# Turning four tiles of an input projection: weight slices stationary, 256 tokens moving

## The reference, cut to what matters

```
h = rmsnorm(x, mix_pre_g)                      # 256 x 2048
proj = h @ w_in                                # 2048 -> 5 * 1024
q, f_logit, i, g, u = split(proj, 5)           # 1024 columns each
f = lb + (1 - lb) * sigmoid(f_logit)           # forget gate, per channel
k = 1 - f
S_t = diag(f_t) S_{t-1} + k_t^T i_t            # 8 heads of 128 channels
o_t = S_t^T q_t
y_rec = rmsnorm(o, g_norm) * silu(g)
```

## Time and profile before

| what | value |
|---|---|
| median of the 3 runs | 1878.26 us |
| lowest and highest | 1876.82 and 1879.6 us |
| profiled execution, first to last instruction | 1875.8 us |
| PE busy in it | 1837.3 us (98%), 8386 matmuls and as many weight loads |
| DVE, ACT, POOL busy | 951.9, 804.5, 49.6 us |
| mean granted TensorE clock | 0.994 of full |

### The profile page before, as it was taken

How to read it: one execution, slowest core, us unless ns; L and a number is a source line. 1 busy time by engine, 2 the same in 40 slices (tenths; PEclk the granted TensorE clock), 3 DMA queues, 4 the chain that set the end, 5 groups by cost and what they waited for, 6 DMA issues and landing times.

```text
span 1875.8 us, 21635 instructions
## 1 busy us (share of the span) xinstructions
PE 1837.3 (98%) x8386; PEld 1525.8 (81%) x8386; DVE 951.9 (51%) x965; ACT 804.5 (43%) x926; POOL 49.6 (3%) x110
## 2 busy tenths in 40 slices
PE   7999999999999999999999999999999999999997
PEld 6888888888788887788888877888888888788886
DVE  4544445544444444655745456445444544444544
ACT  5444444444433434643234445444444444433432
POOL 0000000000000000250000000000000000000000
PEclk9999999999999999999999999999999999999998
DMA  7665656556566656455443554555555655555552
GB/s 263 189 198 180 196 183 192 188 186 194 194 198 191 197 186 199 158 184 176 135 135 131 200 185 149 188 191 189 183 197 182 198 179 191 208 185 201 186 194 90
DMA packets 145438, 344.68 MB, mean 184 GB/s; under 512 B 5400, under 2 KB 5472, under 8 KB 145008
## 3 DMA queue, kind: packets, MB, share of 16 engines
q1 hardware_dynamic: 144544, 339.77, 55.4%
q0 software_dynamic: 736, 4.26, 0.6%
q10 hardware_dynamic: 112, 0.03, 0.0%
HBM read 341.94 MB, written 2.10 MB: 183 GB/s over the span
## 4 chain that ended last, share of the span: by engine, by line
PE 97%; DVE 1%; ACT 1%; POOL 0%; issue 0%; DMA 0%; DVEq 0%; SPq 0%; POOLq 0%; ACTq 0%; PEldq 0%
PE ps L729 31%; PE ps L731 31%; PE ps L730 31%; PE ps L801 1%; PE ps L891 1%; PE ps L783 1%; DVE x L562 0%; PE ps L928 0%; ACT ps L311 0%; DMA x<-in_x_dram 0%; POOL hrr L282 0%; PE ps L918 0%; PE ps L879 0%; DVE xT_lo L488 0%; ACT xT_hi L318 0%
## 5 line engine op out<-in xcount | busy, mean ns | idle before, releaser
L481 DVE TENSOR_TENSOR wlo<-raw,whi 128x1024 fp32r<-128x1024 f32 x640 | 783.0, 1226 | 844.3 <-ACT whi L299 840.3
L299 ACT ACTIVATE whi<-raw 128x1024 fp32r<-128x1024 f32 x640 | 677.7, 1060 | 919.8 <-PE ps L731 918.8
L729 PE MATMUL ps<-whi,xT_hi 128*128 128x512 f32 x1728 | 680.5, 394 | 6.7 <-DVE wlo L481 4.4
L731 PE MATMUL ps<-whi,xT_lo 128*128 128x512 f32 x1728 | 674.9, 391 | 0.0
L730 PE MATMUL ps<-wlo,xT_hi 128*128 128x512 f32 x1728 | 674.6, 390 | 0.0
L729 PEld LDWEIGHTS ps<-whi,xT_hi 128*128 128x128 f32 x1728 | 325.8, 189 | 73.8 <-issue 4.8
L731 PEld LDWEIGHTS ps<-whi,xT_lo 128*128 128x128 f32 x1728 | 325.7, 188 | 68.7
L730 PEld LDWEIGHTS ps<-wlo,xT_hi 128*128 128x128 f32 x1728 | 326.1, 189 | 66.1
L729 PE MATMUL ps<-whi,hT_hi 128*128 128x512 f32 x832 | 324.5, 390 | 2.0 <-PEq L936 1.6
L731 PE MATMUL ps<-whi,hT_lo 128*128 128x512 f32 x832 | 323.7, 389 | 0.0
L730 PE MATMUL ps<-wlo,hT_hi 128*128 128x512 f32 x832 | 323.7, 389 | 0.0
(11 more groups left out here) (99 smaller groups left out, 365.7 us busy)
## 6 DMA issues: line engine op xcount, KB each, us to landing
raw<-in_ffn_w_gate_dram SPq DMA_DIRECT2D x88, 1024.0 KB, 5.2
raw<-in_ffn_w_up_dram SPq DMA_DIRECT2D x88, 1024.0 KB, 5.2
raw<-in_ffn_w_down_dram SPq DMA_DIRECT2D x88, 1024.0 KB, 5.2
raw<-in_w_in_dram SPq DMA_DIRECT2D x40, 1024.0 KB, 5.1
raw<-in_w_out_dram SPq DMA_DIRECT2D x16, 1024.0 KB, 4.9
x<-in_x_dram SPq DMA_DIRECT2D x4, 512.0 KB, 9.3
gpost<-in_ffn_post_g_dram POOLq DMA_DIRECT2D x2, 1024.0 KB, 5.0
out_dram<-x SPq DMA_DIRECT2D x4, 512.0 KB, 2.9
```

The lines of the kernel that those rows point to most:

```text
L299: nc.scalar.activation(whi[:, g % RING, :], raw[:, g // 2 % RAW, 1024 * (g % 2):1024 * (g % 2 + 1)], ACT.Copy).then_inc(hi_ready, 1)
L481: V.tensor_tensor(wlo[:, g % RING, :], raw[:, g // 2 % RAW, 1024 * (g % 2):1024 * (g % 2 + 1)], whi[:, g % RING, :].bitcast(f32), ALU.subt ...
L729: mm(bank, a_hi, whi[:, s, c0:c0 + NT], start=start, stop=False)
L731: return mm(bank, a_lo, whi[:, s, c0:c0 + NT], start=False, stop=stop)
```

## The change

The four first tiles are computed by a new function on PE, with the roles of the operands exchanged: a 128 by 128 slice of `whi` or `wlo` is stationary, and the 256 tokens of `xT_hi` or `xT_lo` move. A half is 24 matmuls of 256 columns. The result has channels on the partitions. The copy into `nat`, the transposes and their evacuation by ACT go for these tiles; DVE takes the banks out, times `rb`, which holds the inverse roots of all 256 tokens on every partition. `rb` is made once: DVE writes `diag` (the identity times each token's root), PE multiplies it by ones (one float32 matmul, 256 columns), ACT copies it out. The sigmoid runs on `T` in place.

```diff
+            def turned_half(g, n, banks):
+                pe.wait_ge(lo_ready, g + 1)
+                s = g % RING
+                for c in range(2):
+                    k = 2 * n + c
+                    for q in range(4):
+                        dst = banks[q // 2][:, SEQ * (q % 2):SEQ * (q % 2 + 1)]
+                        cols = slice(c * NT + P * q, c * NT + P * (q + 1))
+                        mm(dst, whi[:, s, cols], xT_hi[:, k, :], start=k == 0 and q % 2 == 0, stop=False,
+                           skip_group_check=True)
+                        mm(dst, whi[:, s, cols], xT_lo[:, k, :], start=False, stop=False, skip_group_check=True)
+                        ins = mm(dst, wlo[:, s, cols], xT_hi[:, k, :], start=False, stop=k == KC - 1,
+                                 skip_group_check=True)
+                ins.then_inc(w_used, 1)
...
# PE
-                if h == 0 and t >= 2:
-                    pe.wait_ge(nat_ok, 2 * (t - 1))
-                narrow_half(IN + p, 0, h, ps[2 * (t % 2):2 * (t % 2) + 2])
-                if 1 <= t <= 4 and h == 2:
-                    pe.wait_ge(nat_ok, 2 * t)
-                    if t > 1:
-                        pe.wait_ge(in_ev, 2 * (t - 1))
-                    transpose_tile(nat, 0, (4, 5), in_tr, False)
+                if h == 0 and 2 <= t < 6:
+                    pe.wait_ge(in_free, t - 1)
+                if h == 0 and t >= 6:
+                    pe.wait_ge(nat_ok, 2 * (t - 5))
+                if t < 4:
+                    turned_half(IN + p, h, ps[2 * (t % 2):2 * (t % 2) + 2])
+                else:
+                    narrow_half(IN + p, 0, h, ps[2 * (t % 2):2 * (t % 2) + 2])
+                if p == 11:
+                    pe.wait_ge(ones_ok, 1)
+                    pe.wait_ge(diag_ok, 1)
+                    mm(ps[4][:, 0:SEQ], ones[:], diag[:], start=True, stop=True).then_inc(rb_mm, 1)
...
# ACT
-                if 1 <= t <= 4 and h == 4:
-                    act.wait_ge(in_tr, t)
-                    dst, fn = (T, ACT.Sigmoid) if t <= 2 else (qP, ACT.Copy)
-                    h0 = 4 * ((t - 1) % 2)
-                    for c in range(2):
-                        nc.scalar.activation(flat(dst[:, h0 + 2 * c:h0 + 2 * c + 2, :]), ps[4 + c][:],
-                                             fn).then_inc(in_ev, 1)
+                if p == 12:
+                    act.wait_ge(rb_mm, 1)
+                    nc.scalar.activation(rb[:], ps[4][:, 0:SEQ], ACT.Copy).then_inc(rb_ok, 1)
+                if p in (15, 19):
+                    h0 = 0 if p == 15 else 4
+                    for c in range(2):
+                        act.wait_ge(in_tr, h0 // 2 + c + 1)
+                        part = flat(T[:, h0 + 2 * c:h0 + 2 * c + 2, :])
+                        nc.scalar.activation(part, part, ACT.Sigmoid).then_inc(in_ev, 1)
...
-                if h == 7:
+                if h == 7 and t >= 4:
...
# DVE
-                if t in (1, 2) and h == 5:
-                    dve.wait_ge(in_ev, 2 * t)
-                    h0 = 4 * (t - 1)
+                if p == 10:
+                    dve.wait_ge(r_ok, 3)
+                    V.memset(ones[:], 1.0).then_inc(ones_ok, 1)
+                    for b in range(TOK):
+                        ins = V.tensor_scalar(diag[:, P * b:P * (b + 1)], ident[:], rr[:, 2, b:b + 1], None, ALU.mult)
+                    ins.then_inc(diag_ok, 1)
+                if p in (13, 17, 25, 33):
+                    n = p // 8 - 1
+                    dve.wait_ge(w_used, IN + 8 * n + 8)
+                    if n == 0:
+                        dve.wait_ge(rb_ok, 1)
+                    dst, h0, signal = (T if n < 2 else qP), 4 * (n % 2), (in_tr if n < 2 else in_ev)
+                    for c in range(2):
+                        V.tensor_tensor(dst[:, h0 + 2 * c:h0 + 2 * c + 2, :],
+                                        ps[2 * (n % 2) + c][:].rearrange("p (h t) -> p h t", h=2),
+                                        rb[:].unsqueeze(1).broadcast_to([P, 2, SEQ]), ALU.mult).then_inc(signal, 1)
+                    dve.sem_inc(in_free, 1)
+                if p in (17, 21):
+                    dve.wait_ge(in_ev, 2 if p == 17 else 4)
+                    h0 = 0 if p == 17 else 4
```

More of the change, by code:

```diff
@@ L95, in build @@
     vrest = at("vrest", 64, [P, P])
+    rb = at("rb", 200, [P, SEQ])
+    diag = at("diag", 201, [P, SEQ])
+    ones = at("ones", 202, [P, P])
     T = at("T", 64, [P, HEADS, SEQ])
@@ L140, in build @@
         lb_in, lb_exp = sem("lb_in"), sem("lb_exp")
+        ones_ok, diag_ok, rb_mm, rb_ok, in_free = (sem(n) for n in ("ones_ok", "diag_ok", "rb_mm", "rb_ok", "in_free"))
         lev_ready, lev_done, s_last = sem("lev_ready"), sem("lev_done"), sem("s_last")
@@ L434, in _ @@
                     x_hi_part(1, G_MIX, p + 2)
-                if h == 7:
+                if h == 7 and t >= 4:
                     act.wait_ge(w_used, IN + 8 * t + 8)
[L438 to L443, removed]
+                    dst = (v_sb, u_sb, sg)[(t - 4) // 2]
+                    c0 = NT * (t % 2)
                     for b in range(TOK):
@@ L685, in _ @@
                 if p == 75:
-                    dve.wait_ge(nat_ok, 18)
+                    dve.wait_ge(nat_ok, 10)
                     for b in range(TOK):
@@ L702, in _ @@
                 x_after_half(1, 1, G_MIX, p)
-            dve.wait_ge(nat_ok, 20)
+            dve.wait_ge(nat_ok, 12)
             for b in range(TOK):
@@ L902, in _ @@
                     pe.wait_ge(s_last, 2)
-                    pe.wait_ge(nat_ok, 12)
+                    pe.wait_ge(nat_ok, 4)
                     for hh in range(HEADS):
@@ L913, in _ @@
                     pe.wait_ge(orn_ok, 4)
-                    pe.wait_ge(nat_ok, 16)
+                    pe.wait_ge(nat_ok, 8)
                     pe.wait_ge(consts_ok, 1)
@@ L934, in _ @@
                     transpose_tile(orn, 0, (4, 5), yr_tr, False)
-            pe.wait_ge(nat_ok, 20)
+            pe.wait_ge(nat_ok, 12)
             pe.sem_inc(y_free, 4)
```

## The result

The changed kernel takes 1881.11 us (median of 20 runs, 1879.33 to 1882.75), the kernel before 1878.73 us over its 20 runs: a ratio of 1.0014 with a 95% interval of 1.0008 to 1.0021, that is +2.4 us. It is a small loss, inside the 0.2% that was called no change; the forecast was 1880.1, +1.8 us over the median known then, which was that of 3 runs. The profiled execution has a time of 1882.53 us and a span of 1879.4 us.

A forecast was written before the change was run, and what follows sets the result against it. PE, busy 98% of the span, was taken to bound the kernel. Transposes -3.55, exchange +5.1 and `rb` +0.22 us sum to +1.8, taking the median from 1878.26 to 1880.1 us; range 1872.5 to 1885.5.

The forecast's parts named there:

- no change: Whole kernel: time within 0.2%, about 3.8 us, of the kernel before; chance 0.54.
- The place: Tiles 0 to 3, 755 to 866 us: PE has no stall to remove, so only its own instructions count.
- The exchange, +5.1: PE products, tiles 0 to 3: 384 matmuls at 226.7 ns become 768 at 120.1, extra paid per instruction; +5.1 us, chance 0.45.
- The transposes, -3.55: PE, tiles 0 to 3: dropping each tile's 8 transposes saves 0.887 us, all on the path; -3.55 us.
- `rb`, +0.22: PE at p = 11: one added float32 matmul of 256 columns, 216 ns; +0.22 us.
- The waits, 0: New waits at p = 11, 12, 13, 17 cost nothing; DVE at p = 17 tightest. Rival wait 1881 to 1883, chance 0.05.
- In proportion (113.3): Rival, turned products: the extra goes with the columns, step 113.3 ns, exchange 0.0; 1874.9 us, chance 0.18.
- Load slot: Rival, turned products: the weight load's slot is the bound, 110 to 112 ns; 1872.3 to 1873.9 us, chance 0.12.
- Hindrance to 125.4: Rival, turned products: loads and columns hinder each other, step 125.4 ns; 1884.2 us, chance 0.17.
- A pair no closer than 227: Rival, turned products: load and matmul can't follow closer than now, step near 227 ns; 1962 us, chance 0.03.
- The whole, +1.8: Whole kernel: sum of transposes, exchange and `rb`, +1.8 us; span 1875.8 to 1877.6, median 1878.26 to 1880.1.

The follow-up runs named there:

- the merged kernel: Changed kernel with the two matmuls sharing a slice of `whi` made one of 512 columns, sums mixed: 1877.57 us, against 1878.55 for the kernel before.
- the smaller loads: Two kernels: the kernel before with fewer stationary columns (96, 64 or 32) in some tiles, part of the output left out: 1880.03 and 1883.63 us, one run each.
- the first experiment: Kernel before with only the products of tiles 0 to 3 turned, 256 tokens moving, copies and transposes kept: 1883.00 us against 1878.55, ratio 1.0030.
- the rest alone: Changed kernel with the products of tiles 0 to 3 put back to 512 columns moving: 1875.82 us, ratio 0.9986 to the kernel before.
- the kernel with many widths: Kernel before with the moving operand of tiles 1 to 6 cut into widths from 64 to 448 columns: 2097.42 us in one run, against 1877.45.

## Why the prediction was right

**The place.** Right: PE had no stall in the stage before, has none after, and neither the 5.5 us of ACT work nor the DVE work shows.

**The exchange, +5.1.** The choice of 120.1 ns between 110 and 125 decided the sign, and the steps are 120.0. Its ground, an extra that does not shrink with the columns, was shown by the widths 256, 320 and 384 and by the merged kernel. The words "an instruction, or its load, pays once" hold as a price for loads of 128 columns; as a mechanism they were too simple, as the smaller loads showed. The term was too large by 0.7 in the first experiment, 4.44 in the stage. All 384 matmuls had been priced at 226.7 to 120.1. But the first half runs mostly at the lower clock, where the earlier trace rows has no extra to pay (0.16 us of the term), and in that execution the clock rose a little earlier, which is luck (0.14). In the rest of tile 0, seven halves, the exchange added 0.84 us and not 1.12: the old steps there were not 226.7 ns but up to 236 behind each group of transposes of x, while the new ones were back at 120 after four. In tiles 1 to 3 it added 1.22 to 1.26 a tile, where 1.28 was forecast.

**The transposes, -3.55.** Right within 0.1. By the table, a tile without them is 0.89 to 0.93 us shorter (tile 1 with its `rb` taken off), 3.6 in all; the price from the earlier trace rows ends two matmuls behind them, and the old steps are over 226.7 ns for some more.

**`rb`, +0.22.** Wrong by a factor of two: 0.43 in the changed kernel, and 0.48 beside the old products. The forecast took one instruction for one call. The rows it rested on could have told: the 32 rows of L928 are 4 x 2 x 2 = 16 calls in the code. A plain float32 matmul is two in the trace, each at 215.8 ns for 256 columns.

**The waits, 0.** Right, and now with a number: 3.6 us were left at half 20.

**The rivals.** In proportion (113.3): out by the 120. Load slot: it exists, at 111 ns with 128 stationary columns, but lies under the columns' 120. (The eight loads of the earlier trace rows, 1.00 us, are 125 ns each and did not show the 110 that the forecast read beside them; the float32 run did.) Hindrance to 125.4: load and columns do not add up beyond 120. A pair no closer than 227: out. Rules of the Trainium skill, "TensorE: Matmul & The Clock Gate", stood beside two of them. Beside the last, Part 3 has loads overlap running matmuls only in other row groups, and this trace speaks against it with pairs of full-array load and matmul every 120 ns. Beside the load slot, the section "Back-to-back issue gap" gives a formula that makes 109.2 ns for 256 columns and 215.8 for 512, which the section calls the gap of an isolated matmul; the forecast set it against a stream of loads and matmuls. The trace has 120 and 226.7, 11 ns more in both.

**The whole, +1.8.** The stage gave +1.66, and part of that closeness is luck: the products came out lower (about -0.2 beside the other half of the change, -0.7 alone), the transposes saved 0.1 more, `rb` cost 0.2 more, and the first half's +0.17 hangs on when the clock rose. The medians gave +2.4, and the 0.7 beyond the stage is not explained in full. In the single runs the time exceeds the span by 2.13 us in the changed kernel (median of 20) and by 1.74 in the kernel before (23, taken with the experiments), so some 0.4 may lie outside the span, where the forecast had nothing. The clock is the other candidate. The profiled execution of the changed kernel spends 10.2 us at the lower clock around 1127 us, that of before 6.8, and such spells differ between executions of one kernel (its mean granted clock is 0.992 to 0.994 over the 20 runs, its span 1877.2 to 1880.1). The mean over the 20 is 0.9928, and 0.9926 with the products alone (7 runs), against 0.9936 for the kernel before (23) and 0.9937 for the rest alone (11). That points to the 256-column products; no experiment here shows it.

## What to carry to other kernels

When PE is the bound and never waits, price a change of form by the distance of starts, per matmul and load: here 256 moving columns cost 53% of what 512 cost, and turning a product so that it comes out transposed pays only if the transposes it saves (0.9 us a tile) exceed the extra for its doubled instructions (about 1.25 us a tile at the full clock). Keep the moving operand as wide as the bank allows, or merge two matmuls that share a stationary operand. Count instructions in the trace, not calls in the code, and before moving work to an engine that has slack, read how long before its use the next product of that engine is ready.

## What the runs showed that was not expected

- In the kernel with many widths, PE was busy in every microsecond of tiles 5 and 6 and still the granted clock fell from 1.00 to 0.50 with the 64-column matmuls, and stayed there through the mix of 448 and 64 columns; by the estimate above this cost some 120 of the kernel's 220 us. The 128-column matmuls of tile 2, at 111 ns each, had kept it at 1.00. A matmul in the records is not always enough to hold the clock.
- With the clock at the full level, 64 columns were no faster than 128: 111 ns both, with a load of 128 columns each.
- Fewer stationary columns made the step of 512 moving columns longer, not shorter: 226.7 ns with 128, 230 with 96 or 64, 232 with 32, while at 256 moving it went from 120 to 117 and 113. No run here says why.
- A wait of 2.5 us cost 4.3 us, 1.6 of it because the clock fell after it.
